# A convolution layer's diagonal matrices and one of four tap chains on GpSimd

## The reference, cut to what matters

```python
def conformer_conv(glu_in, dw, dw_b, ln_g, ln_b):
    a, gate = jnp.split(glu_in, 2, axis=-1)
    u = a * jax.nn.sigmoid(gate)
    u = lax.conv_general_dilated(
        u, dw[:, None, :].astype(u.dtype), window_strides=(1,),
        padding=[(CONV_WIDTH_2 - 1, 0)], dimension_numbers=('NWC', 'WIO', 'NWC'),
        feature_group_count=CONV_DIM) + dw_b.astype(u.dtype)
    return jax.nn.silu(layer_norm(u, ln_g, ln_b))
```

## Time and profile before

| | |
|---|---|
| time, median of 3 runs | 3255.45 us (3254.53 to 3260.32) |
| the profiled execution's own time | 3255.79 us |
| its span in the profile | 3253.9 us |
| TensorE busy | 3103.9 us (95%) |
| VectorE busy | 2284.1 us (70%) |
| ScalarE busy | 1698.4 us (52%) |
| GpSimd busy | 84.3 us (3%) |
| granted TensorE clock, mean | 0.966 |

### The profile page before, as it was taken

The page is one execution under the profiler, slowest core; times in us unless marked ns, Lnnn a source line. Parts: engine busy times, 40 slices in busy tenths (PEclk is TensorE's granted clock), DMA queues, the critical chain, the costliest instruction groups (busy, mean ns, idle before and its releaser), DMA issues.

```text
span 3253.9 us, 48847 instructions
## 1 busy us (share of the span) xinstructions
PE 3103.9 (95%) x20934; PEld 2865.5 (88%) x20934; DVE 2284.1 (70%) x2612; ACT 1698.4 (52%) x1910; POOL 84.3 (3%) x163
## 2 busy tenths in 40 slices
PE   5999899999988999899989999999999999989999
PEld 5999799999988999899978888888888888889999
DVE  6786668788555555554575898898898888544575
ACT  3434443443534345443435777777777777445453
POOL 1010001011000000000000000000000000000000
PEclk9999999999989999999988999999999999889999
DMA  7685458678422553245412998999999899323353
GB/s 275 245 307 215 149 188 296 225 289 304 156 72 86 213 201 117 78 156 182 155 39 99 368 357 334 367 353 346 355 358 365 336 358 363 142 105 117 114 185 117
DMA packets 112319, 739.23 MB, mean 227 GB/s; under 512 B 12481, under 2 KB 12481, under 8 KB 32097
## 3 DMA queue, kind: packets, MB, share of 16 engines
q1 hardware_dynamic: 89424, 651.21, 53.2%
q0 software_dynamic: 22672, 84.84, 7.4%
HBM read 734.95 MB, written 1.05 MB: 226 GB/s over the span
## 4 chain that ended last, share of the span: by engine, by line
PE 79%; DVE 5%; ACT 2%; issue 1%; DMA 0%; DVEq 0%; ACTq 0%; POOLq 0%
PE ps L515 59%; PE ps L514 18%; PE ps L524 2%; DVE wlo L2704 1%; DVE AF L2686 1%; ACT whi L1824 1%; DVE hl L2677 0%; DVE att L2695 0%; DVE AF L2677 0%; DVE gf L2689 0%; DVE T L2677 0%; ACT cv L1812 0%; ACT hh L1812 0%; ACT L1812 0%; DVE X L2677 0%
## 5 line engine op out<-in xcount | busy, mean ns | idle before, releaser
L2704 DVE TENSOR_TENSOR wlo<-ring,whi 128x2048 fp32r<-128x2048 f32 x620 | 1417.6, 2291 | 466.0 <-ACT whi L1824 465.6
L1824 ACT ACTIVATE whi<-ring 128x2048 fp32r<-128x2048 f32 x620 | 1184.5, 1913 | 336.9 <-issue 222.7
L515 PE MATMUL ps<-whi,AR 128*128 128x512 f32 (+1 forms) x2724 | 878.9, 398 | 0.0
L515 PE MATMUL ps<-hh,whi 128*128 128x256 f32 x2464 | 706.8, 287 | 3.5 <-DVE wlo L2704 3.5
L515 PE MATMUL ps<-hl,whi 128*128 128x256 f32 x2464 | 700.8, 284 | 0.0
L515 PE MATMUL ps<-hh,wlo 128*128 128x256 f32 x2464 | 700.8, 284 | 0.0
L515 PEld LDWEIGHTS ps<-whi,AR 128*128 128x128 f32 x2724 | 510.9, 188 | 117.3 <-DVE AF L2677 0.4
L515 PE MATMUL ps<-wlo,AR 128*128 128x512 f32 (+1 forms) x1362 | 536.2, 394 | 0.0
L515 PEld LDWEIGHTS ps<-hh,whi 128*128 128x128 f32 x2464 | 475.2, 193 | 7.4 <-DVE wlo L2704 3.7
L515 PEld LDWEIGHTS ps<-hl,whi 128*128 128x128 f32 x2464 | 475.1, 193 | 0.5
L515 PEld LDWEIGHTS ps<-hh,wlo 128*128 128x128 f32 x2464 | 474.8, 193 | 0.4
(11 more groups left out here) (219 smaller groups left out, 3262.1 us busy)
## 6 DMA issues: line engine op xcount, KB each, us to landing
ring<-in_w SPq DMA_DIRECT2D x620, 1024.0 KB, 5.0
rring<-in_r POOLq DMA_DIRECT2D x151, 512.0 KB, 4.9
AF<-in_mem POOLq DMA_DIRECT2D x2, 1024.0 KB, 6.3
X<-in_x POOLq DMA_DIRECT2D x1, 1024.0 KB, 14.0
AF<-in_cst POOLq DMA_DIRECT2D x1, 1024.0 KB, 5.3
y_out<-X SPq DMA_DIRECT2D x1, 1024.0 KB, 3.9
cst<-in_cst POOLq DMA_DIRECT2D x1, 608.5 KB, 4.3
sm<-in_small POOLq DMA_DIRECT2D x1, 378.0 KB, 4.5
```

Of the source, the lines that this page charges most:

```text
L515: return self.e.matmul(out, l, r, start=start, stop=stop)
L1824: self.e.activation(N.whi[:, c % HB, :], N.ring[:, c % RING, :], ACT.Copy).then_inc(N.sem["hi"], 1)
L2704: self.e.tensor_tensor(N.wlo[:, c % HB, :], N.ring[:, c % RING, :], N.whi[:, c % HB, :].bitcast(F32), ALU.subtract).then_inc(N.sem["lo"], 1)
```

## The change

GpSimd gets two methods. `diagonals(a, b)` makes the diagonals a to b-1 as `tensor_scalar` (identity times the tap's weight); `taps(j)` makes the 31 taps of tile j. GpSimd makes a tap as two instructions, a product of shifted u and weight into a slot of the scratch T (two slots in turn), and an addition to `c_acc`, which waits for the product. Its `conv_layer` is now: wait for the other engines' marks, diagonals 0 to 33, the taps of tile 3 (once `gated(1)` on VectorE has written its u), diagonals 34 to 61. ScalarE's `diags` is gone. TensorE waits for GpSimd's semaphore where it waited for ScalarE's. VectorE's chains are tiles 0 and 1 in turns, and then tile 2 alone, with 14 taps in each step of the attention where there were 21. The sum over the channels and the layer norm take tile 3 from GpSimd.

```diff
@@ Pe.conv_layer, taps()
-                self.wait_ge("act", ("cv", "dg", n))
+                self.wait_ge("pool", ("cv", "dg", n))
@@ Act.conv_layer
-            diags((8, 13, 13)[i])
@@
             for n in range(3):
-                diags(10)
                 yield
-            diags(2 * TAPS)
@@ Dve.conv_layer
-            for pair in ((0, 1), (2, 3)):
+            for pair in ((0, 1), (2,)):
@@
             for _ in range(4):
-                run(21)
+                run(14)
                 yield
@@
-        run(4 * TAPS)
+        run(3 * TAPS)
@@ Pe and Dve, where the six tiles are summed and read
-            self.wait_ge(*(("dve", ("cv", "conv", j)) if j < 4 else ("act", ("cv", "conv", j))))
+            self.wait_ge(("dve", "dve", "dve", "pool", "act", "act")[j], ("cv", "conv", j))
@@ Pool
     def conv_layer(self):
-        self.fence()
+        self.after()
+        self.diagonals(0, DIAGS)
+        self.taps(3)
+        self.diagonals(DIAGS, 2 * TAPS)
+
+    def taps(self, j):
+        N = self.N
+        a, u, last = N.c_acc[:, j, :], N.c_U[:, j, :], {}
+        self.wait_ge("dve", ("cv", "u", j))
+        for s in range(TAPS):
+            w = N.V("conv_dw_2", 0, TAPS - 1 - s)[:, j:j + 1]
+            if s == 0:
+                self.e.tensor_scalar(a, u, w, N.V("conv_dw_b_2", 0)[:, j:j + 1], ALU.mult, ALU.add).then_inc(*self.up())
+                continue
+            p = N.T[:, 4 + s % 2, 0:S - s]
+            if s > 2:
+                self.wait_ge("pool", last[s % 2])
+            self.e.tensor_scalar(p, u[:, 0:S - s], w, None, ALU.mult).then_inc(*self.up())
+            self.wait_ge("pool", self.here())
+            self.e.tensor_tensor(a[:, s:S], a[:, s:S], p, ALU.add).then_inc(
+                *self.up(*([("cv", "conv", j)] if s == TAPS - 1 else [])))
+            last[s % 2] = self.here()
+
+    def diagonals(self, a, b):
+        N = self.N
+        for d in range(a, b):
+            if d >= DIAGS:
+                self.wait_ge("mm", ("cv", "tapped", d - DIAGS))
+            j, w = 4 + d // TAPS, N.V("conv_dw_2", 0, TAPS - 1 - d % TAPS)
+            self.e.tensor_scalar(N.c_dg[:, d % DIAGS, :], N.ident, w[:, j:j + 1], None, ALU.mult).then_inc(
+                *self.up(("cv", "dg", d)))
```

More of the change, by code:

```diff
@@ L133 @@
 LOADS = ("cst", "small", "x", "mem", "pos", "rot3", "pool3", "mem3")
-SEMS = ("mm", "act", "dve", "hi", "lo", *(f"land{i}" for i in range(RING)), *(f"raw{i}" for i in range(RAW)),
+SEMS = ("mm", "act", "dve", "pool", "hi", "lo", *(f"land{i}" for i in range(RING)), *(f"raw{i}" for i in range(RAW)),
         *("ld_" + n for n in LOADS), "stored", "omm", "oact", "odve", "oland0", "oland1")
@@ L2352, in conv_layer @@
         bi = N.V("conv_b_in_2", 0)
[L2353 to L2364, removed]
         self.chunk()
```

## The result

The changed kernel takes 3269.52 us (median of 6 runs, 3265.69 to 3272.05), the one before 3257.66 us beside it (6 runs, 3254.53 to 3262.25). The ratio is 1.0035, with a 95% interval of 1.0024 to 1.0045: slower, by 11.9 us. Forecast were 3264 us and 9.0 us more. The profiled execution took 3269.36 us, its span is 3267.5.

The account below looks back on a forecast made before the run. TensorE was taken to bound the kernel, waiting in this layer on VectorE's taps. VectorE's slowed path ends the attention 9.0 us later: 3255.8 + 9.0 - 0.3 = 3264.5, stated as 3264 us, range 3244 to 3274.

Parts of the forecast that it names:

- VectorE's slowed taps and copies: Attention: VectorE's last copy done at 1700.5 instead of 1691.5, TensorE's end 8.9 us later at 1709.4, 9.0 later than before.
- The path by GpSimd's chain: Attention's end: chain ends at 1686, plus 18.4 us of TensorE's own work gives 1704.4, hidden under VectorE's 1709.4.
- ScalarE's 1.1 us: Ahead of the attention: without seven diagonals (2.04 us) before a `whi`, VectorE's `wlo` starts 1.1 us earlier.
- A diagonal at 0.34 us: GpSimd's diagonals priced by VectorE's 128 x 128 row; the first 34 take 11.6 us and are covered.
- GpSimd's tap at 1.51 us: Tile 3's chain on GpSimd: a tap costs its own 0.77 us plus two VectorE taps of 0.37.
- turns: GpSimd and VectorE, both reading SBUF, alternate operation by operation; chance 0.45, alone giving 3256 to 3272 us.
- The lower bound: A GpSimd tap takes at least VectorE's durations for the same shapes, 0.35 + 0.42 = 0.77 us.
- VectorE's tap at 0.76 us: VectorE's taps beside GpSimd's chain: 0.76 us each for 0.37, being 0.37 + 0.77 / 2.
- the forecast 6.4: Ahead of the attention: VectorE's 20 slowed taps cost 7.8 us, less 1.1 and 0.3, so it starts at 1660.2.
- Lone taps at 0.52: Tile 2 alone on VectorE: each tap waits for the one before, 0.52 us apart; the last 25 take 13.0 us.
- slow by itself: Rival: no turns, GpSimd's tap up to 1.83 us, attention ends 12.9 us later, kernel 3268 us; chance 0.15.
- The sign named for the forecast: TensorE's 35th tap in the attention would have its diagonal within a few us of wanting it.

Follow-up runs that it names:

- taps_only: The kernel before, with GpSimd making tile 3's taps and ScalarE still the diagonals: 3262.07 us against 3259.78 for the kernel before, ratio 1.0012.
- diagonals_only: The changed kernel, but VectorE keeps all four tiles in pairs and GpSimd makes only the 62 diagonals: 3259.12 us against 3259.78 for the kernel before.
- sum_from_psum: The changed kernel, VectorE's taps reading their second operand from a PSUM bank, output wrong: 3263.08 us against 3258.18 for the kernel before.
- gpsimd_alone: The changed kernel, VectorE making only the first and last tap of its three tiles, output differs: one execution, 3270.59 us against the kernel before's 3258.18.
- tile_left_out: The kernel before, GpSimd making only the first of tile 3's 31 taps, ScalarE the diagonals, output differs: 3245.64 us against 3259.78, ratio 0.9959.
- taps_earlier_2: The kernel before without GpSimd, VectorE's taps regrouped earlier and into its own waits, 18 per attention step: 3247.42 us against 3260.68, ratio 0.9969.

## Why the prediction was right, and where its steps were not

Sign and size were as forecast, +9.0 against +11.9 us, but the term that sets the end was another, and that the numbers agree is in good part luck. The 9.0 came by way of VectorE's slowed taps and copies. That path by itself is worth 3.2 us in the layer and 2.3 in the time (taps_only). The path by GpSimd's chain, which the forecast put at 4.0 us later than before and so hid, gave 14.7. One was priced too high and the other too low, and the forecast took the higher of the two.

**ScalarE's 1.1 us: did not come.** The diagonals ahead of the `whi` are gone, yet VectorE still stands idle for it, as ScalarE's and VectorE's timelines of the changed kernel show:

```profile
1614.55 0.27 ACT L1812 ACTIVATE st<-ps,cst 128x8 f32<-128x8 f32 x1
1617.29 1.91 ACT L1824 ACTIVATE whi<-ring 128x2048 fp32r<-128x2048 f32 x1 [2.47 <-issue]
```

```profile
1617.24 0.88 DVE L2671 SCALAR_TENSOR_TENSOR AF<-ps,sm,gs 128x256 f32<-128x256 f32 x2 [1.68 <-PE ps L515]
1619.23 2.29 DVE L2689 TENSOR_TENSOR wlo<-ring,whi 128x2048 fp32r<-128x2048 f32 x1 [1.11 <-ACT whi L1824]
```

ScalarE idles 2.47 us where the diagonals were. In the order printed ahead of the prediction this `whi` waits for `s_mm` too, and it starts at 1617.29, just as TensorE's last product before it is done, at 1617.20. The profile names no releaser here (`issue`). But the `whi` starts 22.71 us into the layer before, 22.74 after and 22.70 in diagonals_only, with the diagonals and without: they had stood in a wait that was there anyway. diagonals_only shows the same idle 1.11 us on VectorE. I had read the instructions ahead of the `whi` and not its own waits.

**A diagonal at 0.34 us: 0.58 to 0.60, and covered, as said.** The first 34 take 32.15 us for 11.6 forecast, and nothing waits for them. The longest takes 4.67 us, and VectorE's and GpSimd's timelines show two `wlo` beside it:

```profile
1602.10 4.48 DVE L2689 TENSOR_TENSOR wlo<-ring,whi 128x2048 fp32r<-128x2048 f32 x2
```

```profile
1602.38 4.67 POOL L3995 TENSOR_SCALAR AF<-cst,sm 128x128 f32<-128x128 f32 x1
```

Two more, of 2.44 and 2.57 us, start 0.3 us into a single `wlo`. The last 28, with no `wlo` beside them, take 16.24 us and keep ahead of TensorE's taps.

**GpSimd's tap at 1.51 us: 1.78, and made up otherwise.** I had 0.77 for itself and 0.74 for turns. It is 1.62 for itself (sum_from_psum, gpsimd_alone) and 0.16 for VectorE. The lower bound took VectorE's durations; the product alone is 0.93 there, not 0.35. This is the mis-sized term: the chain lasts 57.4 us for 47.8, and starts 1.3 later in the layer than forecast. The sum had a slip besides. In the 7 us in which VectorE rests, nine taps fit at 0.77, which saves 6.7 us against 1.51 and not 3.4; the chain would have been forecast at 1683, still further under VectorE's path.

**VectorE's tap at 0.76 us: 0.58 to 0.63.** The wait ahead of the attention grew by 4.15 us, its start came 4.2 later in the layer for the forecast 6.4. Lone taps at 0.52 are 0.50 undisturbed; the forecast had them undisturbed, but GpSimd was still at its chain, and they came every 0.60 us.

**Which path decides.** I had VectorE's copies end last (1709.4) and hid the chain under them (1704.4). VectorE is done with its taps at 1698.6 (1695.5 in the forecast's count, for 1699.9), and every us of the chain shows: 18.4 us behind it was the forecast, 18.2 came, and 17.6 in sum_from_psum and gpsimd_alone. So the mechanism at the end is that of the rival "slow by itself", with its long wait for a diagonal. The sign named for the forecast, a 35th diagonal within a few us of wanting it, failed by 11.55 us. In sum_from_psum and gpsimd_alone, where VectorE's taps disturb nothing, the layer is 5.8 to 6.2 us shorter than the changed kernel's, and still 8.5 to 8.9 longer than before. The chain took 57.4 / 31 = 1.85 us a tap, as much as that rival's highest price, but only 1.62 is GpSimd's own, and the rest is contention: both are in the result.

**Turns.** The Trainium skill, page "SBUF — State Buffer", section "Who interferes with whom", has VectorE with two SBUF operands and GpSimd exclude each other for an instruction's length. The trace agrees at `wlo`, and sum_from_psum at the operand count. Strict turns between short instructions it does not show: then VectorE's spacing would be near my 0.76, and it is 0.58 to 0.63. The page "GPSIMD Engine Reference", section "Performance versus the Vector engine", gave an estimated 0.53 us for an addition of 241 elements; the trace has 0.61. It has no price of this product.

**The account of the layer,** from kernel to kernel: -9.3 us if tile 3 simply left VectorE (tile_left_out); +12.5 for its taps on GpSimd, through VectorE's slower taps (taps_only); +11.5 for the 28 diagonals behind GpSimd's chain. That is the +14.7. By the times the same steps are -14.1, +16.4 and +9.6, together +11.9: each step is sure in its sign, and its size only to some us.

## What to carry to other kernels

Moving work to an engine that stands idle pays only if what it costs the others, per instruction, is less than what it frees: here 0.42 us of VectorE against the 0.26 that a tap given up really freed, since the tile left behind lost its partner. What stands behind the moved chain in the new engine's queue is late by the whole chain; look there for what TensorE wants first. And before moving work off an engine that is waited for at certain points, try to place it between those points: the order of the same taps gave 10 to 13 us, in taps_earlier_2 about half of it as shorter waits and half as a higher clock between them.

## What the runs showed of the hardware

- GpSimd's TENSOR_SCALAR with one operation took 0.93 to 0.94 us for 128 x 254 and 255, with a second one (plus 0.0) 0.49 for 128 x 255. The simpler form is the slower.
- VectorE's 128 x 2048 instruction with two SBUF operands held up a GpSimd instruction nearly for its whole length (0.63 to 2.35 us, 1.08 to 3.20, a diagonal 0.60 to 4.67 beside two of them) and lost nothing itself.
- Between short instructions both lost: VectorE 0.21 to 0.25 us per tap in turns and 0.10 per lone tap, GpSimd 0.16 us per tap at the head of its chain. Over the whole chain GpSimd lost 5.5 us (57.4 for 51.9 in sum_from_psum) and VectorE 12.7. With GpSimd's shorter product VectorE lost more still, its ten taps 7.23 us for 6.39, and a `wlo` 2.71 for 2.29.
- In the 5 us behind TensorE's wait of 11.55 us its granted clock was 0.51, and six taps took 5.12 us where ten took 4.31 at 1.00. In taps_earlier_2, with no wait over 1.6 us in the attention, it stayed at 1.00. That the waits make the difference is read from the traces, and no run tests it by itself.
- With its second operand in PSUM VectorE neither lost nor took any of this.
